# Feed-forward block: first down tile no longer waits for the last inner tile, second down chunk split right behind it, splitting work of the up weights spread out

## What is computed

```
def _conv_ffn(x, norm_g, w_up, conv_w, conv_b, w_down):
    h = _rmsnorm(x, norm_g)
    up = h @ w_up
    gate, val = up[..., :D_FF], up[..., D_FF:]
    gate = lax.conv_general_dilated(gate, conv_w[:, None, :].astype(gate.dtype), window_strides=(1,),
                                    padding='SAME', dimension_numbers=('NWC', 'WIO', 'NWC'),
                                    feature_group_count=D_FF) + conv_b
    return (jax.nn.silu(gate) * val) @ w_down
...
        x = x + _conv_ffn(x, ffn_norm[layer], ffn_w_up[layer], ffn_conv_w[layer], ffn_conv_b[layer],
                          ffn_w_down[layer])
```

## Time and profile before

| | us |
|---|---|
| median of 3 runs | 2407.09 (2404.88 to 2409.62) |
| the profiled execution | 2411.21 |
| its span, first to last instruction | 2409.4 |
| PE busy | 2260.3, 94% of the span |
| DVE, ACT, POOL busy | 1296.1, 1242.2, 213.5 |
| mean granted TensorE clock | 0.981 of full speed |

### The profile page before, as it was taken

One profiled execution on the slowest core, in us unless ns is written; L12 is line 12 of the kernel. 1 busy time (PEld: TensorE's weight loads), 2 busy tenths in 40 slices (PEclk: granted clock), 3 DMA queues, 4 the chain that ended last, 5 costly groups with the idle time before them and its releaser, 6 DMA issues.

```text
span 2409.4 us, 30092 instructions
## 1 busy us (share of the span) xinstructions
PE 2260.3 (94%) x11736; PEld 1088.5 (45%) x11736; DVE 1296.1 (54%) x2596; ACT 1242.2 (52%) x2209; POOL 213.5 (9%) x288
## 2 busy tenths in 40 slices
PE   7999999999999999999999999989996999989995
PEld 3434544444444444444444446554333444654333
DVE  5565855546455546776654584653225644643223
ACT  7544656666547565566665863622225664421212
POOL 0000000000000430000000000011221000101231
PEclk9999999999999999999999999999998999999997
DMA  5220011221222110222223231549974231338995
GB/s 197 88 107 1 1 71 70 105 105 73 96 103 108 70 70 36 104 91 103 83 77 125 84 101 49 203 148 378 418 295 155 77 140 39 160 114 334 415 425 229
DMA packets 68590, 340.33 MB, mean 141 GB/s; under 512 B 11766, under 2 KB 12076, under 8 KB 54092
## 3 DMA queue, kind: packets, MB, share of 16 engines
q1 hardware_dynamic: 51408, 267.67, 28.8%
q0 software_dynamic: 17040, 70.74, 7.7%
HBM read 368.72 MB, written 23.10 MB: 163 GB/s over the span
## 4 chain that ended last, share of the span: by engine, by line
PE 81%; DVE 9%; ACT 5%; issue 3%; DMA 2%; POOL 0%; DVEq 0%; SPq 0%; POOLq 0%; ACTq 0%
PE PB L383 11%; PE PB L388 11%; PE PB L389 11%; PE PB L3255 9%; PE PB L3281 4%; PE PB L1677 3%; PE PB L1673 3%; PE PB L1674 3%; PE PB L408 2%; PE PB L410 2%; PE PB L409 2%; PE PB L419 2%; PE PB L3207 1%; DVE WS L320 1%; ACT junk L261 1%
## 5 line engine op out<-in xcount | busy, mean ns | idle before, releaser
L388 PE MATMUL PB<-AS,WS 128*128 128x512 f16 x1416 | 537.0, 379 | 16.7 <-ACT AS L478 12.7
L389 PE MATMUL PB<-AS,WS 128*128 128x512 f16 x1416 | 536.7, 379 | 0.0
L383 PE MATMUL PB<-AS,WS 128*128 128x512 f16 x1416 | 508.4, 379 | 2.6 <-DVE AS L1150 2.5
L320 DVE SCALAR_TENSOR_TENSOR WS<-raw,sc,WS 128x1024 f16<-128x1024 f32 (+3 forms) x288 | 324.4, 1187 | 91.8 <-ACT WS L307 91.8
L307 ACT ACTIVATE WS<-raw,sc 128x1024 f16<-128x1024 f32 (+3 forms) x288 | 284.3, 1056 | 64.4 <-DVE sc L287 64.4
L261 ACT ACTIVATE junk<-raw 128x1024 f16<-128x1024 f32 (+3 forms) x288 | 280.6, 974 | 9.7 <-DMA raw<-in_w_out_even 0.7
L3255 PE MATMUL PB<-T 128*64 128x512 f32 x736 | 218.1, 603 | 22.9 <-issue 17.5
L388 PEld LDWEIGHTS PB<-AS,WS 128*128 128x128 f16 x1416 | 138.5, 98 | 196.3 <-ACT AS L478 22.4
L383 PEld LDWEIGHTS PB<-AS,WS 128*128 128x128 f16 x1416 | 138.5, 98 | 172.2 <-DVE AS L1150 4.1
L389 PEld LDWEIGHTS PB<-AS,WS 128*128 128x128 f16 x1416 | 138.6, 98 | 162.8 <-issue 3.0
L296 DVE TENSOR_REDUCE sc<-sc 128x1 f32<-128x4 f32 x72 | 11.3, 156 | 273.9 <-POOL sc L275 273.9
(11 more groups left out here) (628 smaller groups left out, 3510.2 us busy)
## 6 DMA issues: line engine op xcount, KB each, us to landing
T<-in_moe_up SPq DMA_DIRECT2D x26, 2048.0 KB, 10.9
raw<-in_w_up SPq DMA_DIRECT2D x22, 2048.0 KB, 7.7
T<-in_moe_down SPq DMA_DIRECT2D x26, 1024.0 KB, 13.1
raw<-in_w_down SPq DMA_DIRECT2D x16, 1408.0 KB, 6.0
raw<-in_w_in_even SPq DMA_DIRECT2D x8, 2048.0 KB, 7.8
raw<-in_w_in_odd SPq DMA_DIRECT2D x8, 2048.0 KB, 7.8
moe_y<-X SPq DMA_DIRECT2D x30, 512.0 KB
WS<-in_moe_up SPq DMA_DIRECT2D x6, 2048.0 KB
```

Source lines behind the costliest of these rows:

```text
L320: e.scalar_tensor_tensor(lo[q], raw[q], s, hi[q], MUL, SUB).then_inc(*k.s("dve_split").up("lo", i, q))
L383: return e.matmul(bank, wh[:, q, c, :], act.lo[c], start=False, stop=c == kt - 1)
L388: e.matmul(bank, wh[:, q, c, :], act.hi[c], start=c == 0, stop=False)
L389: e.matmul(bank, wl[:, q, c, :], act.hi[c], start=False, stop=False)
```

## The change

It has four parts.

1. PE no longer waits for `hid(21)` in front of the first down tile, and the 10 and the 6 matmuls without result are gone. The first two down tiles wait at inner tile 16 for the last readers of PB0 and PB1 (`conv(20)` and `hid(20)`).
2. In the up phase the squares and quarters of the next chunk are spread out: two squares on each side of a gate's silu, two `hi` quarters behind the square sum of the second tile, one each in front of and behind the silu of the third. DVE's scale and first two `lo` quarters come behind the second tile's `hid`, the other two behind the third tile's taps.
3. The squares of the second down chunk come in front of the square sum of `hid(21)`; its scale comes right behind `total(1)`, its quarters 0 and 1 in front of the halves 16 to 21, its quarters 2 and 3 behind them.
4. POOL's sum for that chunk stands in front of the total of group 1. `act_out` and `dve_down` leave the second chunk out.

```diff
@@ act_out @@
-        act_ahead(k, e, w, name, t)
+        if t >= made:
+            act_ahead(k, e, w, name, t)
@@ ffn_pool @@
         pool_ahead(k, e, w, m.up, tiles)
+        if g:
+            pool_sum(k, e, w, place(m.down, 1)[0])
@@ ffn_pe @@
     def free(bank):
-        w.wait_ge(*v.past("hid", FF - 1))
         if layer:
             w.wait_ge(*k.s("act_ffn1").past("s5_turn", 0))
-
-    pe_out(k, e, w, m.stage, m.down, m.parts, m.then, free, pe_down, 10)
+            w.wait_ge(*v.past("s5_turn", 0))
+            w.wait_ge(*v.past("s5_kern"))
+
+    def down(k, e, w, name, t, act, bank, first):
+        pe_down(k, e, w, name, t, act, bank, first, (v.past("conv", FF - 2), v.past("hid", FF - 2)))
+
+    pe_out(k, e, w, m.stage, m.down, m.parts, m.then, free, down)
@@ pe_down @@
-        if c == EARLY and t >= 2:
-            w.wait_ge(*act.sig.past("out", t - 2))
-        if c == EARLY and first:
-            pe_warm(k, e, late[:, 0:128], 6)
+        if c == EARLY:
+            w.wait_ge(*(act.sig.past("out", t - 2) if t >= 2 else read[t]))
@@ ffn_act @@
+    def gate(i):
+        w.wait_ge(*v.past("conv", i))
+        e.activation(m.cv[i % 3], m.cv[i % 3], ACT.Silu).then_inc(*a.up("gate", i))
+
     for t in range(2 * FF):
-        act_ahead(k, e, w, m.up, t)
         i = t // 2
         c = m.cv[i % 3]
+        n, q = place(m.up, t)
+        if t == 0:
+            act_squares(k, e, w, n + 1)
...
-            w.wait_ge(*v.past("conv", i))
-            e.activation(c, c, ACT.Silu).then_inc(*a.up("gate", i))
+            if q == 0 and t:
+                act_square(k, e, w, n + 1, 0)
+                act_square(k, e, w, n + 1, 1)
+            if q == 2:
+                act_hi_quarter(k, e, w, n + 1, 2)
+            gate(i)
+            if q == 0 and t:
+                act_square(k, e, w, n + 1, 2)
+                act_square(k, e, w, n + 1, 3)
+            if q == 2:
+                act_hi_quarter(k, e, w, n + 1, 3)
         else:
+            if t == 2 * FF - 1:
+                act_squares(k, e, w, n + 2)
             w.wait_ge(*v.past("hid", i))
             act_square_sum(k, e, w, i, m.hid[i], m.stage, "hid", i)
+            if q == 1:
+                act_hi_quarter(k, e, w, n + 1, 0)
+                act_hi_quarter(k, e, w, n + 1, 1)
...
+    second = place(m.down, 1)[0]
+    for j in (0, 1):
+        act_hi_quarter(k, e, w, second, j)
     for i in range(EARLY, FF):
         hi(i)
+    for j in (2, 3):
+        act_hi_quarter(k, e, w, second, j)
     e.preload_act_table_set(LN_EXP)
-    act_out(k, e, w, m.stage, m.down, m.then)
+    act_out(k, e, w, m.stage, m.down, m.then, 1)
@@ ffn_dve @@
-            dve_scale(k, e, w, place(m.up, t)[0] + 1)
-        if t % 4 == 1:
-            dve_lo(k, e, w, place(m.up, t)[0] + 1)
...
+        if t % 4 == 1:
+            dve_scale(k, e, w, place(m.up, t)[0] + 1)
+        if t % 4 in (1, 2):
+            for j in range(2):
+                dve_lo_quarter(k, e, w, place(m.up, t)[0] + 1, 2 * (t % 4 - 1) + j)
...
     total(1)
+    second = place(m.down, 1)[0]
+    dve_scale(k, e, w, second)
     for i in EARLY_PARTS[2 * FF - 1]:
         lo(i)
     scale(1)
+    for j in (0, 1):
+        dve_lo_quarter(k, e, w, second, j)
     for i in range(EARLY, FF):
         lo(i)
+    for j in (2, 3):
+        dve_lo_quarter(k, e, w, second, j)
     dve_down(k, e, w, m)
```

More of the change, by code:

```diff
@@ L547, in pe_out, with act_out @@
         pe_warm(k, e, k.PB[OUT_BANKS[0]][:, 0:128], 13)
-def act_out(k, e, w, stage, name, then):
+def act_out(k, e, w, stage, name, then, made=0):
     v, a = k.s(f"dve_{stage}"), k.s(f"act_{stage}")
     for t in range(8):
-        act_ahead(k, e, w, name, t)
+        if t >= made:
+            act_ahead(k, e, w, name, t)
         if then == "rms":
@@ L1636, in ffn_pool @@
             *k.s(f"pool_{m.stage}").up("total", "hid", g))
-    pool_ahead(k, e, w, m.down, range(8))
+    pool_ahead(k, e, w, m.down, range(1, 8))
 def ffn_pe(k, e, w, layer):
@@ L1651, in free, with pe_down @@
     def free(bank):
-        w.wait_ge(*v.past("hid", FF - 1))
         if layer:
             w.wait_ge(*k.s("act_ffn1").past("s5_turn", 0))
-    pe_out(k, e, w, m.stage, m.down, m.parts, m.then, free, pe_down, 10)
-def pe_down(k, e, w, name, t, act, bank, first):
+            w.wait_ge(*v.past("s5_turn", 0))
[3 more added lines that the diff above has]
+    pe_out(k, e, w, m.stage, m.down, m.parts, m.then, free, down)
+def pe_down(k, e, w, name, t, act, bank, first, read):
     i, _ = place(name, t)
@@ L1800, in dve_down @@
     for t in range(8):
-        dve_ahead(k, e, w, m.down, t, m.parts)
+        if t:
+            dve_ahead(k, e, w, m.down, t, m.parts)
+        else:
+            dve_tile_scale(k, e, w, m.down, t, m.parts)
         i, out = place(m.down, t)[0], k.x[t]
```

## The result

| | median, us | runs | against before on the same chip, 95% interval |
|---|---|---|---|
| before | 2407.09 | 5 | |
| changed | 2394.76 (2390.95 to 2397.45) | 5 | 0.9941 (0.9926 to 0.9956) |

The change saves 12.3 us by the medians, 0.51%, and 0.59% by the ratio. Forecast were 14.3 us, 2392.8 us and faster; the time is inside the range of 2387.5 to 2400.5. The profiled execution took 2392.47 us, its span 2390.7 us, which is 18.7 us less than the span of before.

What follows compares the result with a forecast made beforehand. PE, with 81% of the chain of waits, was taken as the bound: 8.43 us a layer removed, less a new 1.28 us wait, gains 14.3 us in two layers, 2407.09 to 2392.8 us; range 2387.5 to 2400.5.

Steps and rivals of the forecast that it cites:

- What goes: PE at the seam from up to down phase: idling and empty matmuls vanish, at most 8.43 us a layer, 16.9 in two.
- First down chunk, no wait: Start of the first down tile: the chunk's last `lo` quarter ends 589.72, 0.2 us early, so PE does not wait.
- The chain behind: ACT at the seam: `hi(14)` waits for `lo(11)`, four squares follow, `hid(21)`'s square sum begins at 594.70, adding 1.5 us.
- DVE's row of work: DVE from 595.49: 9.88 us without gaps, second down chunk ready at 605.43, PE waits 1.28 us before the second down tile.
- The clock: PE at the seam: the low-clock windows go, and the new 1.28 us wait lowers no clock; nothing charged.
- Edits at nothing: Up phase and later: spread squares and quarters, later loads and the third down chunk cost PE nothing.
- The cases that did not come: Alternatives: no wait 2390.2 us (0.19); longer wait, lower clock 2398.2 (0.17); gain absorbed 2407 (0.06); slower 2412.9 (0.04).
- absorbed: Behind the seams: something other than PE sets the end, so the gain is lost, 2407 us; chance 0.06.
- the slower case: Second down chunk's load lands after 598.1, delaying squares and `hid(21)`'s square sum; 2412.9 us at a landing at 601; chance 0.04.
- The sum: Whole kernel: 7.14 us a layer, 14.3 us in two, off the median 2407.09, giving 2392.8 us; chance 0.54.

Runs made afterwards that it cites:

- hi14_later: Changed kernel with `hi(14)` and `lo(14)` moved from up tile 42 to 43, behind which the second down chunk's squares no longer stand; ratio 0.9939 against before.
- no_warm: Kernel before without its 10 and 6 empty matmuls, nothing else changed; 2.5 us faster than before, ratio 0.9987.
- pe_only: Kernel before with part 1 alone: no wait for `hid(21)`, no empty matmuls, old splitting order; 0.8 us slower than before, ratio 1.0003.
- changed_again: The changed kernel measured again, nothing altered; 2395.36 us against 2409.81 for before, ratio 0.9929.
- split_only: Changed kernel with before's wait for `hid(21)` and empty matmuls restored, so parts 2 to 4 alone; 4.8 us faster than before, ratio 0.9968.
- spread_undone: Changed kernel with part 2 undone: up-phase squares, quarters and scale where before had them; 9.0 us faster than before, ratio 0.9961.
- warm_kept: Changed kernel with the 10 empty matmuls put back before the first down tile, without any wait; 11.2 us faster than before, ratio 0.9953.

## Why the prediction was right, point by point

- **What goes.** 8.43 us a layer, 7.10 in front of the first tile and 1.33 within it: hi14_later, where nothing waits, shows 8.43.
- **First down chunk, no wait.** Forecast in before's time were silu at 587.28 and the last `lo` quarter's start at 588.79 with 0.2 us to spare. In the changed trace, whose up tile 43 ends 0.62 us earlier, they are at 586.68 and 588.11, both within 0.1 us when that is taken off, and PE doesn't wait. That quarter ends at 589.06 and the first down matmul starts at 589.28, so the margin was as thin as forecast, 0.2 us.
- **The chain behind.** `hi(14)` behind `lo(11)`, then squares, then the square sum at 594.70 - 0.62 = 594.08: measured 594.09 (fences above). That it was the head of the path is shown by hi14_later, which takes this link alone out and loses the wait.
- **DVE's row of work.** Forecast 9.88 us from `total(1)` to the end of the last quarter. Its sum, 595.49 + 9.88, is 605.37; the 605.43 that it goes on with has 0.06 us more, which it does not explain, and the changed kernel shows 0.05 from the row's end to PE's start (604.53 to 604.58). The changed kernel's timeline of DVE:

```profile
594.85 0.16 DVE L1776 TENSOR_REDUCE small<-small 128x1 f32<-128x6 f32 x1 [2.47 <-ACT junk L443]
594.92 0.15 DVE L296 TENSOR_REDUCE sc<-sc 128x1 f32<-128x4 f32 x1
...
597.03 1.80 DVE L320 SCALAR_TENSOR_TENSOR WS<-raw,sc,WS 128x704 f16<-128x704 f32 x2
598.74 4.06 DVE L1784 SCALAR_TENSOR_TENSOR T<-T,sc 128x512 f16<-128x512 f32 x6
602.72 1.81 DVE L320 SCALAR_TENSOR_TENSOR WS<-raw,sc,WS 128x704 f16<-128x704 f32 x2
```

  It ends at 604.53, after 9.68 us. `total(1)` holds DVE 0.07 us and not 0.16, and the two scales and `lo(15)` together 2.11 instead of 2.24. These 0.2 us are why the wait is 1.06 us and not 1.28, and a layer gains 7.37 instead of 7.14.
- **The clock.** No fall over the new wait, as charged. The price put on a fall was too low for a long one: 0.4 x 3.8 = 1.5 us was read from a burst behind 3.2 us of idling. Behind as much it was 1.4 and 1.7 us (no_warm), and behind 6.9 us it was 2.7 and 2.0 (pe_only). The forecast did not hang on it, since the clock stayed.
- **Edits at nothing.** In the up phase PE never waits in the changed kernel either: from 360 to 720 us its list of waits has the start of the phase and of the next layer, where PE waits for the norm, and the wait at tile 1 only.
- **The cases that did not come.** Nothing was absorbed behind the seams: the marker behind the second layer is 15.4 us earlier. The second chunk's load, forecast for about 571, was issued at 570.16 in the changed trace, and such loads land 5.8 to 6.4 us later, 14 us before the first square at 590.39. Its landing was not varied, so the slower case is shown only not to have happened, not how it would go.
- **The sum.** 14.3 forecast, 14.7 in the two seams of the trace, 12.3 and 14.5 by the medians of two groups of runs. In the table the medians gain less than the seams say in seven of eight rows, by 0.1 to 2.4 us, and in pe_only the kernel loses 1.1 us less. The recorded ratios don't bear out such a lean: changed_again (17.1 us by its ratio), split_only (7.7) and no_warm (3.1) gain more than their seams, changed (14.2), spread_undone (9.4), warm_kept (11.3) and hi14_later (14.7) less. The traces put the difference outside the first block. So that 12.3 came out 2 us under the forecast says nothing against its terms, and a median nearer to it would have said as little for them; the seams do.

## What to carry to other kernels

Where one engine is nearly always busy, draw up the deadlines behind a wait before removing it, and add up the other engines' instructions to each: here removing the wait alone gained nothing, because the next chunk took its place one tile later and the clock fell in that wait. Look in such a chain for links by a reused buffer (`hi(14)` behind `lo(11)`): they put a whole run of unrelated work, here four squares of weights, behind a small instruction. Empty matmuls that keep the clock up are to be priced at what the wait costs without them: 3.77 us of them here replaced a loss of 1.4 to 1.7.

## What the runs showed of the hardware

The granted clock and PE's idle time in front of it go together, but what a fall costs differs, also between the two layers of one run. After 0.9 us (changed) and after 2.17 and 1.88 us of idling (no_warm's second wait in the two layers) matmuls went on with a start each 0.216 us, the 2.4 GHz level; after 1.67 us (split_only) the granted clock was 1.00 as well. After 3.2 us (no_warm) seven started 0.43 us apart in layer 0, the 1.2 GHz level, and eight in layer 1, where three had still followed at the full level. After 6.9 us (pe_only) it was thirteen in layer 0 and ten in layer 1. The loss behind the idle time was 1.4 and 1.7 us in the first case, 2.7 and 2.0 us in the second: an idle time twice as long cost not only itself but also more behind it.

The same 10 empty float32 matmuls took 3.77 us after 3.17 us of idling, 2.33 after 1.67, and 2.23 with none. In a row of the trace a matmul at the lower level lasts 0.61 to 0.63 us against 0.38, which finds such places without the windows.
